# Products of zeros in nine waits of TensorE, and the denominators' transposes ahead of the value products

## What is computed

```python
def first_block(...):
    for i in range(DEPTH):                       # DEPTH = 2
        h = h + 0.5 * swiglu(rmsnorm(h, norm_ffn1[i]), ffn1_w_gate[i], ffn1_w_up[i], ffn1_w_down[i])
        hn = rmsnorm(h, norm_mix[i])
        j = i // 2
        if i % 2 == 0:
            h = h + ab_mixer(hn, w_in_ab[j], sink_a[j], w_out_ab[j], pos)
        else:
            h = h + c_mixer(hn, w_in_c[j], rpb_c[j], w_out_c[j])
        h = h + 0.5 * swiglu(rmsnorm(h, norm_ffn2[i]), ffn2_w_gate[i], ffn2_w_up[i], ffn2_w_down[i])
        gate = jax.nn.sigmoid(rmsnorm(h, norm_ple[i]) @ w_ple_gate[i])
        h = h + gate * (p[i] @ w_ple_proj[i])
    return rmsnorm(h, norm_final)

def second_block(...):
    h = rmsnorm_2(x, norm1_g[l]) * (1.0 + sc1) + sh1
    ... = jnp.split(h @ w_in[l], offsets, axis=-1)
    o_hg = hgrn2_mixer(...)
    o_nsa = nsa_mixer(...)
    x = x + g1 * (jnp.concatenate([o_hg, o_nsa], axis=-1) @ w_out[l])
    h = rmsnorm_2(x, norm2_g[l]) * (1.0 + sc2) + sh2
    x = x + g2 * moe_ffn(h, ...)                 # 8 of 64 experts a token, and a shared one
    return rmsnorm_2(x, final_g)
```

## Time and profile before

| | us |
|---|---|
| median of 3 runs | 3309.93 |
| lowest, highest | 3309.85, 3315.95 |
| the profiled execution's own time | 3311.66 |
| its span, first to last instruction | 3309.8 |
| mean granted clock of PE, share of full | 0.994 |

### The profile page before, as it was taken

One profiled execution on the slowest core, in us unless ns is written; L12 is line 12 of the kernel. 1 busy time (PEld: TensorE's weight loads), 2 busy tenths in 40 slices (PEclk: granted clock), 3 DMA queues, 4 the chain that ended last, 5 costly groups with the idle time before them and its releaser, 6 DMA issues.

```text
span 3309.8 us, 48007 instructions
## 1 busy us (share of the span) xinstructions
PE 3236.2 (98%) x16206; PEld 2607.8 (79%) x16206; DVE 1931.5 (58%) x2444; ACT 1718.0 (52%) x2077; POOL 1340.1 (40%) x677
## 2 busy tenths in 40 slices
PE   8999999999999999999999999999989999999998
PEld 7888887678888788888778888778866788888884
DVE  4335684663355433461374333347667899999997
ACT  5552334545533555331445542423363788888884
POOL 3444442044444344444324444434302444454441
PEclk9999999999999999999999999999999999999999
DMA  3224331022244222443422223223103999999997
GB/s 128 95 96 164 127 105 58 8 91 100 95 146 150 85 95 95 141 155 110 128 83 101 96 93 98 100 76 106 65 7 125 360 377 385 386 391 387 377 371 299
DMA packets 128449, 534.37 MB, mean 161 GB/s; under 512 B 24432, under 2 KB 24688, under 8 KB 100464
## 3 DMA queue, kind: packets, MB, share of 16 engines
q1 hardware_dynamic: 107488, 499.63, 42.2%
q0 software_dynamic: 20736, 33.60, 2.7%
q10 hardware_dynamic: 144, 0.08, 0.0%
HBM read 531.64 MB, written 41.94 MB: 173 GB/s over the span
## 4 chain that ended last, share of the span: by engine, by line
PE 74%; issue 14%; DVE 5%; POOL 5%; ACT 1%; DMA 1%; POOLq 0%; DVEq 0%; SPq 0%; ACTq 0%
PE ps L883 21%; PE ps L885 21%; PE ps L884 20%; POOL w_lo L2107 5%; PE ps L1456 2%; PE ps L1072 1%; PE ps L903 1%; PE ps L1082 1%; PE ps L1097 1%; PE ps L1202 1%; PE ps L1240 1%; PE ps L1155 0%; PE ps L1475 0%; DVE x_lo L2281 0%; PE ps L1163 0%
## 5 line engine op out<-in xcount | busy, mean ns | idle before, releaser
L2107 POOL TENSOR_TENSOR w_lo<-stage_buf,w_hi 128x1024 fp32r<-128x1024 f32 (+1 forms) x396 | 968.8, 2447 | 1329.9 <-ACT w_hi L1637 1329.9
L1637 ACT ACTIVATE w_hi<-stage_buf 128x1024 fp32r<-128x1024 f32 (+1 forms) x396 | 414.2, 1046 | 1180.6 <-PE ps L885 1125.5
L883 PE MATMUL ps<-x_hi,w_hi 128*128 128x512 f32 x1984 | 773.3, 390 | 4.0 <-POOL w_lo L2107 2.3
L885 PE MATMUL ps<-x_hi,w_lo 128*128 128x512 f32 x1984 | 772.0, 389 | 0.0
L884 PE MATMUL ps<-x_lo,w_hi 128*128 128x512 f32 x1984 | 771.9, 389 | 0.0
L883 PE MATMUL ps<-hid,w_hi 128*128 128x512 f32 x1312 | 518.5, 395 | 2.8 <-issue 1.7
L885 PE MATMUL ps<-hid,w_lo 128*128 128x512 f32 x1312 | 511.6, 390 | 0.0
L884 PE MATMUL ps<-hid,w_hi 128*128 128x512 f32 x1312 | 510.8, 389 | 0.0
L883 PEld LDWEIGHTS ps<-x_hi,w_hi 128*128 128x128 f32 x1984 | 372.4, 188 | 85.2 <-POOL w_lo L2107 4.1
L885 PEld LDWEIGHTS ps<-x_hi,w_lo 128*128 128x128 f32 x1984 | 372.4, 188 | 77.7
L884 PEld LDWEIGHTS ps<-x_lo,w_hi 128*128 128x128 f32 x1984 | 372.4, 188 | 76.7
(11 more groups left out here) (411 smaller groups left out, 4789.2 us busy)
## 6 DMA issues: line engine op xcount, KB each, us to landing
stage_buf<-in_gu SPq DMA_DIRECT2D x176, 512.0 KB, 3.2
big<-in_exp_gu SPq DMA_DIRECT2D x72, 1024.0 KB, 10.1
h_buf<-in_exp_gu SPq DMA_DIRECT2D x72, 1024.0 KB, 9.9
s_buf<-in_exp_dn SPq DMA_DIRECT2D x72, 1024.0 KB, 9.5
stage_buf<-in_down SPq DMA_DIRECT2D x64, 512.0 KB, 3.6
stage_buf<-in_down SPq DMA_DIRECT2D x32, 384.0 KB, 3.2
sil_buf<-in_ada SPq DMA_DIRECT2D x24, 512.0 KB, 4.2
tmp_buf<-in_ada SPq DMA_DIRECT2D x24, 512.0 KB, 4.3
```

What stands on the lines that cost most here:

```text
L883: nc.tensor.matmul(o, a_hi, b_hi, start=start, stop=False)
L885: return nc.tensor.matmul(o, a_lo, b_hi, start=False, stop=stop)
L1637: nc.scalar.activation(w_hi[s][:, 0:n], stage[s][:, 0:n], ACT.Copy).then_inc(upper_done, 1)
L2107: nc.gpsimd.tensor_tensor(w_lo[s][:, 0:n], stage[s][:, 0:n], w_hi[s][:, 0:n].bitcast(F32), ALU.subtract).then_inc(parted, 1)
```

## The change

`keep_clock` is called at nine more places on PE (score steps 29 and 30 counted as one): 8 products after the last unit of each of the two folded attentions, ahead of the wait for the last copy by ACT; 14 between `weighted_sum` and `spread_factor`; 4 ahead of score steps 29 and 30 of the recurrence and 8 after its 32 steps; in `gated` 10 ahead of the transposes of units 0 and 3, and 20 ahead of those of unit 15, the last; 36 in the final sum, after the shared expert's products and ahead of the first wait for a late row. The transposes of a pair's denominators leave `values` and stand in a function of their own, `spread`, which PE runs just before the value products of the pair's last unit (in `c`: of its last two units) instead of just after them. DVE's multiplication at line 2513 waits for the value products of the unit as well, since the copy of the denominators no longer implies them.

```diff
--- before.py
+++ after.py
@@ -1097,8 +1097,11 @@
                         last = nc.tensor.matmul(ps[64 * hf:64 * hf + 64, 6 + un["pair"] % 2, un["t"] * P:un["t"] * P + P], v,
                                                 turned_of(name, j)[:, c * P:c * P + P], start=(c < 2), stop=(c >= nk - 2))
                     last.then_inc(fo["pv"], 1)
+
+                def spread(j):
+                    un = units[j]
                     if un["last"]:
-                        k = un["spread"][0]
+                        n, k = a["pairs"] + un["pair"], un["spread"][0]
                         pe.wait_ge(fo["rden_wide"], n + 1)
                         bank_free(k)
                         for t in range(TT):
@@ -1117,8 +1120,10 @@
                         for j in range(i - 2, i - 2 + step):
                             turn(j)
                     if i >= late:
+                        spread(i - late + step - 1)
                         for j in range(i - late, i - late + step):
                             values(j)
+                keep_clock(2, 8)
                 pe.wait_ge(evacuated["act"], units[-1]["spread"][2])
 
             def head_sum(hd):
@@ -1177,9 +1182,14 @@
                     if 2 <= i <= len(units) + 1:
                         j = i - 2
                         un = units[j]
-                        if j == 2:
+                        if j == 0:
+                            keep_clock(4, 10)
+                        elif j in (2, 3):
                             pe.wait_ge(att["pts"], un["pieces"][0] - 1)
-                            keep_clock(4 + un["pieces"][0] % 2, 24)
+                            keep_clock(4 + un["pieces"][0] % 2, 24 if j == 2 else 10)
+                        elif j == len(units) - 1:
+                            pe.wait_ge(att["sc_read"], 4 * len(units))
+                            keep_clock(0, 20)
                         pe.wait_ge(att["probs"], j + 1)
                         for m, k in enumerate(un["pieces"]):
                             turn(k, [n_s[j % 3][:, a:a + P] for _, a, _ in un["chunks"][4 * m:4 * m + 4]])
@@ -1291,6 +1301,8 @@
                     last.then_inc(hg["pv"], 1)
 
                 for i in range(32):
+                    if i in (29, 30):
+                        keep_clock(2, 4)
                     scores(i)
                     if i < 16:
                         compress_step(2 * i)
@@ -1533,6 +1546,7 @@
                     add(t, 2).then_inc(fin["part"], 1)
                 shared_down(1, False)
                 shared_down(2, False)
+                keep_clock(0, 36, add=True)
                 for t in range(TT):
                     if t == 3:
                         shared_down(t, False)
@@ -1585,6 +1599,7 @@
                 elif st == "mix_2":
                     pe.wait_ge(evac_done, u("in_2") + 1)
                     weighted_sum()
+                    keep_clock(4, 14)
                     spread_factor("norm1")
                     dense("in_2", "norm1")
                     norm_sum("first")
@@ -2503,6 +2518,7 @@
                     if i >= 5 and units[i - 5]["last"]:
                         un = units[i - 5]
                         dve.wait_ge(fo["pts_act"], un["spread"][2])
+                        dve.wait_ge(fo["pv"], at + i - 4)
                         o, rd, m = ps[:, 6 + un["pair"] % 2, :], r_sb, mixed[:, un["pair"], :]
                         if name == "c":
                             o, rd = (x.rearrange("p (c r) -> p c r", r=8) for x in (o, rd))
```

## The result

The changed kernel has a median of 3316.77 us over 22 runs (3305.65 to 3324.59), the kernel before 3310.12 over 22 runs beside them (one of these, of 6929 us, is left out of its mean). The ratio is 1.0019, with a 95% interval of 1.0013 to 1.0025: slower by 0.19%, clear of the scatter but small. (The prediction took 0.2%, a time above 3316.5 us, as the least that can be told; the ratio lies just short of that, the median 0.3 us beyond it.) The means say the same: 3316.7 against 3311.1, +5.6 us with a standard error of 1.2. Forecast were 3305.5 and a range up to 3312.5, so direction, size and range were wrong.

What follows compares the result with a forecast made beforehand. PE, busy 98% of the span, was taken as the bound. Terms summed to -5.4 us, giving 3306.3 from the profiled 3311.66 or 3304.5 from the median 3309.93; it took 3305.5, range 3300.0 to 3312.5.

Steps and rivals of the forecast that it cites:

- The clock terms: Prevented clock falls at both attention ends, `in_2`, the recurrence and the sparse attention: 7.15 us of gain in all.
- falls come by chance: Rival, chance 0.27: a run of before has on average half the falls, so clock terms are worth half; 3308.1 us.
- That zero products don't hold the clock: Rival, chance 0.08: at all nine waits clock terms vanish and products on the path cost time; 3314.3 us.
- The norm: 14 products ahead of `spread_factor`: 0.94 us on the path, about 1.35 us back in `in_2`; net -0.4 us.
- Unit 15's twenty: Twenty products ahead of the sparse attention's last unit, where PE does not wait, stand on the path: +2.1 us.
- The order in `ab`: In `ab`'s loop PE waits for the bank first where its second kind of pair begins, values after: +0.3 us.
- In `c`: In `c`'s loop a new 0.3 us stall per pair, against ACT's exponentials coming 0.47 us sooner: +0.3 us.
- The ends of the attentions: `ab` and `c` ends: DVE starts 0.63 us earlier, eight products hidden, clock kept (1.6 us each): -4.4 us.
- The recurrence and the sparse attention: Recurrence products hidden, low stretch at 2367.2 gone, -1.7 us; tens ahead of units 0 and 3 paid back or hidden, -0.9 us.
- The final sum: 36 products hidden in a 5.58 us DMA wait; first eight products at line 1523 end earlier: -0.7 us.

Runs made afterwards that it cites:

- e1: The changed kernel without its new zero products (new order alone); mean +1.5 us against the kernel before, ratio 1.0004.
- e4: The kernel before with only the 36 zero products of the final sum added; mean 0.0 us against before, ratio 0.9998.
- e5: The kernel before plus zero products at the norm (14), ahead of unit 0 (10) and unit 15 (20); +4.3 us, ratio 1.0013.
- e8: The kernel before with the new order at each attention's last pair only, no new zero products; -0.3 us, ratio 0.9999.
- e9: The kernel before plus ten zero products ahead of each of units 3, 6, 10 and 14 of the sparse attention; +0.1 us, ratio 0.9999.
- e10: The kernel before with its own zero products taken out; +9.7 us, ratio 1.0029.
- e12: The kernel before plus 60 zero products ahead of unit 15's transposes; +8.0 us, ratio 1.0024.
- e6: The kernel before plus the change's zero products except those at the norm, unit 0 and unit 15; -0.9 us, ratio 0.9999.
- e11: The kernel before plus last-pair new order and zero products at attention ends, recurrence, units 3, 6, 10, 14 and final sum; 3305.79 us, ratio 0.9985.
- e2: The kernel before with all the change's zero products, in its own order; +5.1 us, ratio 1.0019.
- e13: e11 plus the change's 14 zero products at the norm; +0.9 us against the kernel before, ratio 1.0006.
- e15: e11 plus the change's 20 zero products ahead of unit 15; -1.5 us against the kernel before, ratio 0.9998.
- e14: e11 with the new order in all pairs; -2.4 us against the kernel before, ratio 0.9991.
- e3: The changed kernel without the 36 zero products of the final sum; +5.3 us against the kernel before, ratio 1.0017.

## Why the prediction was wrong

**The clock terms, the step that failed most.** 7.15 us of gain were booked as a fall prevented here and there, since one trace of before had falls there. Two of these falls carried 3.2 us of the sum, those behind the ends of `ab` and `c` (646.9 and 1684.6), a third 1.7 us, that at 2367.3. Seven other traces are without zero products at these places (e1, e4, e5, e8, e9, e10, e12): one of them, e12's, had the first, none the second, and in none does a fall begin between 2350 and 2375. On average before loses 14.6 to 16.1 us to the clock, by the group of runs, and the changed kernel 14.9: 0.1 us less than the 15.0 of the first group, in place of 7.15. The text had this as a rival, "falls come by chance", with 0.27, and put it at 3308.1, so even that lay 8.7 us below the result: it halved the gain and left the costs as they were.

**That zero products don't hold the clock** (0.08, 3314.3) gave a time near to the result, by a mechanism that is not there: e10 shows 11.1 us more of clock lost without them, and e6 and e11 lose less than before. That they hold the clock and that the changed kernel gains none go together: three of the places bring none (e5: 15.7 against 14.6 us), and at three of the others, the two ends and the recurrence, hardly a trace has a fall without them.

**The norm (-0.4; bounds -1.3 and +2.4).** The gain rested on the clock staying up in `in_2`. The fall came all the same, in every one of the seventeen traces between 2152 and 2160, with the 14 products or without: in five of the six traces with the 14 the clock falls before or among them, in e2's 3.6 us behind their last, soon after the wait for `x_hi`. The upper bound said what then happens, 14 x 0.21 - 0.57 = 2.4 us; the traces show 0.9 to 2.7 us at `spread_factor` and 1.5 on average in `in_2`, and e13 a total of 5.6 (1.5). The value was taken at the wrong end, although and the low stretch of the earlier trace rows already stood for the low clock right behind these sums.

**Unit 15's twenty (+2.1; 0 to 4.2).** Right, mechanism and size: 2.2 us of timeline with no idle, 2.0 net against a PE at the full clock, 2.7 per twenty in e12, 3.2 (1.3) in e15. In the trace of the changed kernel only 1.3 us of it can be read as a difference, for before ran this stretch at the lower clock.

**The order in `ab` (+0.3; 0 to 0.6).** The step that failed is "in `ab`'s plain pairs the piece before last belongs to the unit whose values follow anyway": true, but the pairs of three pieces wait for DVE's copy of theirs, and that copy stands behind four reductions. Each such wait grows from 0.53 us or from none to 1.11 us, and the end of the pairs comes 1.9 us later, three times the upper bound. **In `c`** (+0.3; -0.5 to +2.1) 0.15 us in each of six pairs, +0.9, is inside the bounds, and both sides of the balance are there: the stall of 0.34 us, and ACT's exponentials that come sooner, for which 1.4 us comes back at the last pair. e14 has 2.3 us for all of the order against the last pair's alone.

**The ends of the attentions (-4.4; -5 to -1.3).** The mechanism is as told (copy made early, DVE right behind the last values, eight products hidden), and 0.5 us of the 0.63 is seen at `ab`. The two clock terms of 1.6 us each weren't there to be had on average, see above: here the terms that failed are the clock's, not the copy's. e8, which has this copy and no zero product, measured -0.3 (0.8): -1.3 is not excluded, and not shown.

**The recurrence and the sparse attention.** The 4 + 4 + 8 products and unit 3's ten are hidden, as said: at 2367 the trace goes from step to step without delay. The ten ahead of unit 0 took 1.3 us, 0.4 of it at the lower clock, and the wait behind them shrank from 1.39 to 0.29 us. What was not foreseen are low stretches of 10 to 14 us during the small products between 2334 and 2390, in five of the seventeen traces (e1, e2, e3, e10, e15), with and without new zero products. No filler stands inside these products. The same group of unit 0's scores in e2's trace, at the lower clock, and in the changed kernel's, mostly at the full one (one of its 64 products is listed apart):

```profile
2376.85 7.08 PE L1173 MATMUL ps<-big 64*128 64x32 f32 x64
```

```profile
2377.02 3.75 PE L1177 MATMUL ps<-big 64*128 64x32 f32 x63
```

**The final sum (-0.7).** The clock stayed up behind the 36, as said. That they are hidden holds where the earlier wait is short; no run shows the gain clear of noise (e3, e4). That this earlier wait has falls of its own was not in the prediction.

**The sum with measured terms.** Places on the path +4.3 (e5), order +1.5 to +2.3 (e1, e14), places in waits -0.9 (e6): +4.9 to +5.7 us, against +5.6 measured, with a standard error of some 1.8 us, so that the agreement is closer than it has a right to be. Read off the traces instead: the order +1.9 - 0.5 in `ab` and +0.9 - 1.4 in `c`, the 14 +1.5, the twenty +2.1, together +4.5 us, and nothing for the clock.

One statement of the Trainium skill (TensorE: Matmul & The Clock Gate, Part 1) was cited for the rival that came nearest in mechanism, falls by chance: that the window of the activity monitor runs free of the kernel. The runs agree with what follows from it: the mean granted clock of the changed kernel goes from 0.993 to 0.998 over its 22 executions, and the executions of one kernel scatter by 1.4 to 4.8 us in standard deviation.

**What stays open.** Why the 14 cost 5.6 us in e13 where 2.1 is seen in its trace and 1.5 in the average one: a shift of later falls, or chance (its executions scatter by 4.1 us). And why PE waits in the expert loop in some executions, for expert weights as I take it (the profile names no engine for most of these waits): PE waited up to 3.9 us in the expert loop (2600 to 3255) in e9's trace, 3.0 in e1's, 0.8 in the changed kernel's and 0.3 in e6's; no experiment touched that. A single trace is off by that much before any change is read from it. These waits don't swallow what is gained earlier: over the seventeen traces the time at which `out_2` begins (2460 to 2476 us) and the span (3302 to 3318) go together, with a correlation of 0.93.

## What to carry to other kernels

Don't book a fall of the clock as a loss that can be recovered because one trace has it: compare the mean granted clock over many executions, and count a place only if the fall is there in most traces. A filler pays in a wait that is longer than it and that is followed by a fall in most traces (the late wait of the final sum, four waits of the sparse attention); on the path it costs its whole length (2 to 3 us for twenty here), and behind the norm's sums it ran at the lower clock in most traces and saved nothing. When an instruction is moved forward in a queue, list for each kind of turn (plain, three pieces, last) whose result it now waits for, and what that result is queued behind.

## What the runs showed of the hardware

- At the norm the clock fell between 2152 and 2160 in all seventeen traces, though PE had hardly been idle. What PE had just done: twelve products with a stationary operand of one column (5.2 us), then 24 products with one moving column (3 us). Which of the two the fall goes with isn't shown. Fourteen zero products behind them didn't prevent it, not even in e2's trace, where all fourteen ran at the full clock and it fell at 2159.7.
- The stretch from 2330 to 2390, where PE is busy for 54 to 58 of 60 us with mostly small products (16 to 128 columns), had low stretches of 10 to 14 us in five traces.
- Zero products in bf16 hold the clock in a wait. Without the kernel's own, 27.2 us of clock were lost instead of 16.1, and it took 9.7 us longer. With ten in each of four waits of the sparse attention no trace of five has a fall there, without them ten of twelve; with 36 in the late wait of the final sum none of nine, without them seven of eight.
- A place has its fall in some executions only. 2579.1 in the changed kernel's trace and 2578.2 in e4's had one, and no other trace near it; 646.9 had one in before's and e12's, 1684.6 in before's alone. The mean time of the changed kernel is 5.6 us above its own profiled execution.
